# Reordering the recurrent stage of a hybrid decoder step: lagged page values, sample tokens inside turns, twelve value places

## The chip, the cores and the metric

The kernel runs on one core of one Trainium2 chip. The metric is device time in microseconds (us) of one execution. The engines are named as the profile names them: PE (TensorE matmul), PEld (its weight load), DVE (VectorE), ACT (ScalarE), POOL (GpSimd) and SP (SyncE, which issues DMAs only). Each engine executes its own queue strictly in the order in which the program wrote it; semaphores join the queues.

## The reference, cut to what matters

One inference step of a two-layer decoder trunk, for 1024 prompt tokens and 8 sample tokens with the same weights. Layer 0 joins stick-breaking attention and a matrix-state recurrence (RWKV-7) in one projection; layer 1 is a gated DeltaNet; each layer ends in a convolutional feed-forward part. The change is in layer 0's recurrent stage, in which two things are computed side by side.

```python
# (a) the recurrence, 8 heads, state 64 x 64 per head, over the 1024 prompt tokens, and one step for each sample
def step(s, inp):
    r_t, w_t, k_t, v_t, kk_t, a_t = inp
    sa = einsum('bhvk,bhk->bhv', s, kk_t)
    s = s * w_t - sa (x) (kk_t * a_t) + v_t (x) k_t
    return s, einsum('bhvk,bhk->bhv', s, r_t)
# then per head: group norm of o, + bonus = sum(r*k*r_k) * v, times the gate g = sigmoid(xg) @ g_up

# (b) stick-breaking attention of each sample token over 8192 past positions in 64 pages of 128
z = q . k * scale + bias                      # 64 key pages, 8 heads
u = log_sigmoid(-z); after = reverse cumulative sum(u) - u
w = exp(log_sigmoid(z) + after)
o = sum over pages of w @ v                   # 64 value pages
```

## The kernel before, in words

The recurrent stage is `rwkv_phase` (L1367). It cuts the 1024 prompt tokens into NPAIR = 8 blocks of W = 128 tokens and runs turns i = 0 to 8. In turn i, block i is "local": its Gram matrices are formed, and a triangular system is solved by doubling in five levels (`solve_y`, `solve_z`, DVE `level`, L2027). Block i-1 is "walked": the state is read, changed and multiplied out in two half steps p = 0, 1 (`state_read`, `new_values`, `change_and_outputs`, DVE `state`, L2036), then normed and gated (`center`, `normed`, `outputs`). Block i+1 is "prepared": gates, decays and keys are computed (`gate_ones` to `bonus`, DVE). The semaphore `solved` is counted by the DVE's last `level` (the second L2034 row of level 5), and PE's next `turn` (transposes, L1507) waits for it.

Between these steps lie the samples' cache pages, one sample per turn. A page is 128 positions x 512 floats, 256 KB.

- Key pages: SP loads them into 8 places (`load_keys`, L1008). DVE multiplies two pages by the sample's query (L1103) and sums (L1106) into scores `pg_z`. Such a pair is a unit; a turn takes KEYS_TURN = 26 units, spread by calls `more(n)`, the rest after the last level. All 256 units are done before turn 7; turn 6 gets the last 18.
- Page weights: DVE adds the bias (L1118), ACT takes three activations (`logs_act`, L1072 to L1074), DVE forms the softplus `pg_sp` (L1123), PE two running sums (`sums_pe`, L1030 and L1031), DVE four operations (`exponents_dve`, L1130 to L1133), and ACT the exponential `pg_w` (L1078). Sample i+1's weights are made at the end of turn i; sample 0's before turn 0.
- Value pages: POOL loads them into RING = 8 places (`load_values`, L1060, DMA at L1065), each behind a wait for the place's release by PE. PE multiplies four pages at a time (`values_pe`, L1035, matmul L1044; `more(4)` in PE's list). Sample i's 64 pages are all multiplied in turn i, the rest after the last `solve_z`. Then ACT copies the sum out (`fold_act`, L1083, which waits for the 64th page), PE selects (L1051, `select_pe`), and ACT picks (L1090), all before the next turn's transposes.

POOL also loads each block's projected rows X (L1456), from one place in its list; the first one, the LoRA weights and the first eight value pages are loaded once the stage has begun.

The 8 sample tokens are a ninth block. It is prepared in turn 7. After turn 7's last value page its rows are transposed (L1639), copied, written to memory and read back in another layout (SP, L1432 to L1437); nine DVE operations make its state step (L1931 on `pg_k`, L2160, L2167), and the result goes through memory again (L1443, L1447) to be normed, gated and written to `h`. Then the output projection (`residual_phase`) begins.

What stands between "engine", "line" and "operation" in a row is the program's name of the tile; many DVE operations go through the helper `tt` and so all bear L1931.

Of the kernel before, what the change touches and what calls it, by code (L numbers as in the profile page):

```python
# [14 lines left out]
F32 = mybir.dt.float32  # L15
# [6 lines left out]
P = 128  # L22
D_MODEL = 1024
SEQ = 1024
# [931 lines left out]
class Pages:  # L956
# [3 lines left out]
    RING = 8  # L960
    ZRING = 4
    UNITS = NPG // 2

    def __init__(self, T, ctx):
# [4 lines left out]
        self.v_in = [sems(f"v_in{n}") for n in range(self.RING)]  # L969
# [7 lines left out]
        self.kp, self.vp = sb("_k", [P, self.RING, D_A]), sb("_v", [P, self.RING, D_A])  # L977
# [5 lines left out]
        self.zb, self.sp, self.tmp, self.cum = (sb(n, [P, H_A * NPG]) for n in ("_zb", "_sp", "_tmp", "_cum"))  # L983
# [4 lines left out]


# [31 lines left out]
    def start_pe(self, pe):  # L1021
        pe.wait_ge(self.qc_in, 16)
        for t in range(4):
            mm = pe.transpose(self.T.ps[0:NS, 7, t * P:(t + 1) * P], self.qc[:, t, :], self.T.const("ident"))
        mm.then_inc(self.q_turned, 1)
        pe.sem_inc(self.v_used, self.RING)
# [6 lines left out]
    def values_pe(self, pe, b, pages):  # L1033

        wts = self.wts[:, b % 2, :].rearrange("p (h n) -> p h n", h=H_A)  # L1035
        for at in range(0, len(pages), 4):
            four = pages[at:at + 4]
            if four[0] == 0:
                pe.wait_ge(self.w_ready, b + 1)
            for g in four:  # L1040
                pe.wait_ge(self.v_in[g % self.RING], 16 * (NPG // self.RING * b + g // self.RING) + 16)
            for g in four:
                c = 32 * (g % 4)
                pe.matmul(self.T.ps[c:c + H_A, 7, :], wts[:, :, g], self.vp[:, g % self.RING, :], start=(g < 4),  # L1044
                          stop=(g >= NPG - 4), tile_position=(0, c), skip_group_check=True).then_inc(self.v_used, 1)
# [15 lines left out]
    def load_values(self, pool, b, g):  # L1061

        pool.wait_ge(self.v_used, NPG * b + g + 1)
        page = pool.value_load(self.table[0:1, NPG * b + g:NPG * b + g + 1], min_val=0, max_val=self.T.n_phys - 1)
        pool.dma_start(self.vp[:, g % self.RING, :], self.T.io["v_pages"][bass.ds(page, 1), :, :]  # L1065
                       .rearrange("a p n -> (a p) n")).then_inc(self.v_in[g % self.RING], 16)

    def logs_act(self, act, b):
# [3 lines left out]
        st.link(act.activation(self.tmp[:, :], self.zb[:, :], ACT.Abs))  # L1072
        st.link(act.activation(self.tmp[:, :], self.tmp[:, :], ACT.Exp, scale=-1.0))
        act.activation(self.tmp[:, :], self.tmp[:, :], ACT.Ln, bias=1.0).then_inc(self.logged, 1)  # L1074

    def weights_act(self, act, b):
        act.wait_ge(self.z_ready, b + 1)
        act.activation(self.wts[:, b % 2, :], self.cum[:, :], ACT.Exp).then_inc(self.w_ready, 1)  # L1078

    def fold_act(self, act, b):  # L1080
        act.wait_ge(self.v_used, self.RING + NPG * b + NPG)
# [33 lines left out]
    def bias_dve(self, dve, b):  # L1115
        assert self.unit >= self.UNITS * (b + 1)
        dve.wait_ge(self.reduced, self.UNITS * (b + 1) + 1)
        dve.tensor_tensor(self.zb[:, :].rearrange("p (h n) -> p h n", h=H_A), self.z[:, b % self.ZRING, :, :],  # L1118
                          self.T.vec("sb_bias").unsqueeze(2).to_broadcast([P, H_A, NPG]), ALU.add).then_inc(self.biased, 1)

    def softplus_dve(self, dve, b):
        dve.wait_ge(self.logged, b + 1)
        dve.scalar_tensor_tensor(out=self.sp[:, :], in0=self.zb[:, :], scalar=0.0, in1=self.tmp[:, :], op0=ALU.max,  # L1123
                                 op1=ALU.add).then_inc(self.softplus_ready, 1)

    def exponents_dve(self, dve, b):

        st, ps, run = Steps(dve, self.step, 3 * b), self.T.ps, self.tmp[:, :]
        dve.wait_ge(self.summed, b + 1)
        st.do(dve.tensor_tensor(self.cum[:, :], self.zb[:, :], ps[:, 6, :], ALU.subtract))  # L1130
        st.link(dve.tensor_tensor_scan(run, self.T.const("scanhead"), ps[:, 5, :], 0.0, ALU.mult, ALU.add))
        st.link(dve.tensor_tensor(run, run, ps[:, 5, :], ALU.subtract))
        dve.tensor_tensor(self.cum[:, :], self.cum[:, :], run, ALU.subtract).then_inc(self.z_ready, 1)  # L1133


KEYS_V, KEYS_PB, KEYS_ATT, KEYS_TURN = 16, 42, 24, 26


def attention_phase(T):
# [23 lines left out]
    with ExitStack() as ctx:  # L1163
# [12 lines left out]
        def _(pool):  # L1176
            for i in range(2):
                for u in range(2):
# [9 lines left out]
                      .then_inc(heads_in[u], 16)  # L1188

# [176 lines left out]

def rwkv_phase(T):  # L1367

# [1701 lines left out]
```

## Time and profile before

| | |
|---|---|
| three timed runs | 4803.83, 4805.32 (median), 4811.03 us |
| the profiled execution's own time | 4802.16 us |
| its span, first to last instruction | 4800.6 us |
| mean granted PE clock | 0.869 of 2.4 GHz |
| busy over the span | PE 3889.0, PEld 3356.1, DVE 2353.2, ACT 1177.8, POOL 399.9 us |
| the recurrent stage | about 697 to 1713 us of the span |
| value page DMAs, key page DMAs | 512 of 256 KB each kind, landing in 4.6 and 4.3 us (medians) |

Rows of the trace give a start and a duration in us from the span's start. An idle time in square brackets is that of the engine just before the row, with what ended it. PE's clock is the granted share of 2.4 GHz in a stretch, and takes the levels 1.2 and 2.4 GHz. A matmul row may join several instructions ("x8"), since an fp32 matmul is issued in two passes.

### The profile page before, as it was taken

The numbers are of one execution on the slowest core, as the hardware profiler recorded it, in microseconds if no ns is written. First come the engines' busy times: TensorE is split into PE (matmuls) and PEld (weight loads), VectorE is DVE, ScalarE is ACT, GpSimd is POOL, SyncE is SP. The second block draws the span as 40 slices with busy tenths as digits, with TensorE's granted clock in tenths as the row PEclk, the third lists the DMA queues.
The fourth block names the chain that finished last, engine by engine and source line by source line (L and its number), as shares of the span: only waits on it lengthen the run. The fifth ranks groups of instructions, "written<-read, shape, count | busy, mean of one in ns | idle before, by whom it ended". The sixth has DMA issues, their size and how long they took to land. (4 is left out here: it accounts for less than half of the span.)

```text
span 4800.6 us, 77677 instructions
## 1 busy us (share of the span) xinstructions
PE 3889.0 (81%) x29645; PEld 3356.1 (70%) x29645; DVE 2353.2 (49%) x3055; ACT 1177.8 (25%) x1872; POOL 399.9 (8%) x737
## 2 busy tenths in 40 slices
PE   6897875666666766999999699969888376999999
PEld 5695323344344466999999589857777276999999
DVE  2488878777775243344421345444444533434511
ACT  3223661222222112222310222222222012222300
POOL 0010003223223100000000000000000000000000
PEclk8998987777778688999999899977777588999999
DMA  2464227788776322111122222211010132111122
GB/s 95 154 208 148 75 72 262 267 270 271 270 267 219 105 102 76 51 46 44 45 76 69 96 89 80 85 45 36 19 36 10 43 137 75 44 44 53 43 77 66
DMA packets 212082, 512.43 MB, mean 107 GB/s; under 512 B 34129, under 2 KB 67297, under 8 KB 205274
## 3 DMA queue, kind: packets, MB, share of 16 engines
q1 hardware_dynamic: 149338, 305.83, 19.6%
q0 software_dynamic: 62496, 203.32, 12.4%
q8 instruction: 152, 2.49, 0.2%
q14 instruction: 96, 0.79, 0.0%
HBM read 454.87 MB, written 54.56 MB: 106 GB/s over the span
## 5 line engine op out<-in xcount | busy, mean ns | idle before, releaser
L263 PE MATMUL ps<-ffn_hh,up_wh 128*128 128x344 f32 x2112 | 678.3, 321 | 59.6 <-DVE up_wl L255 59.6
L265 PE MATMUL ps<-ffn_hl,up_wh 128*128 128x344 f32 x2112 | 676.7, 320 | 0.0
L264 PE MATMUL ps<-ffn_hh,up_wl 128*128 128x344 f32 x2112 | 675.9, 320 | 0.0
L263 PEld LDWEIGHTS ps<-ffn_hh,up_wh 128*128 128x128 f32 x2112 | 398.5, 189 | 60.7 <-issue 60.7
L265 PEld LDWEIGHTS ps<-ffn_hl,up_wh 128*128 128x128 f32 x2112 | 398.4, 189 | 0.0
L264 PEld LDWEIGHTS ps<-ffn_hh,up_wl 128*128 128x128 f32 x2112 | 398.4, 189 | 0.0
L458 PE MATMUL ps<-down_ah,down_wh 128*128 128x344 f32 x1056 | 343.2, 325 | 29.6 <-DVE down_al L492 18.1
L459 PE MATMUL ps<-down_ah,down_wl 128*128 128x344 f32 x1056 | 340.0, 322 | 0.0
L460 PE MATMUL ps<-down_al,down_wh 128*128 128x344 f32 x1056 | 339.9, 322 | 0.0
L1103 DVE TENSOR_TENSOR pg_prod<-pg_k,pg_q 128x1024 f32<-128x1024 f32 x256 | 313.4, 1224 | 40.0 <-DVE rw_mxt L2034 10.7
L1065 POOL DMA_DIRECT2D pg_v<-in_v_pages x512 | 275.8, 539 | 601.9 <-issue 467.0
L1106 DVE TENSOR_REDUCE pg_z<-pg_prod 128x16 f32<-128x1024 f32 x256 | 312.9, 1222 | 8.8
L1044 PE MATMUL ps<-pg_v,pg_w 128*8 128x512 f32 x1024 | 170.3, 747 | 173.2 <-DMA pg_v<-in_v_pages 170.5
L263 PE MATMUL ps<-hh,odd_wh 128*128 128x344 f32 x792 | 258.4, 326 | 63.9 <-DVE odd_wl L255 63.9
L265 PE MATMUL ps<-hl,odd_wh 128*128 128x344 f32 x792 | 254.9, 322 | 0.0
L264 PE MATMUL ps<-hh,odd_wl 128*128 128x344 f32 x792 | 254.8, 322 | 0.0
L458 PEld LDWEIGHTS ps<-down_ah,down_wh 128*128 128x128 f32 x1056 | 200.6, 190 | 34.2 <-issue 29.2
L459 PEld LDWEIGHTS ps<-down_ah,down_wl 128*128 128x128 f32 x1056 | 201.6, 191 | 0.0
L263 PEld LDWEIGHTS ps<-hh,odd_wh 128*128 128x128 f32 x792 | 150.5, 190 | 72.6 <-ACT odd_row L2233 42.0
L460 PEld LDWEIGHTS ps<-down_al,down_wh 128*128 128x128 f32 x1056 | 200.7, 190 | 0.0
L255 DVE TENSOR_TENSOR down_wl<-down_w,down_wh 128x896 fp32r<-128x896 f32 (+1 forms) x48 | 54.3, 1135 | 280.2 <-ACT down_wh L250 280.2
L663 DVE TENSOR_TENSOR ffn_a<-up_cv,ps 128x344 f32 (+1 forms) x132 | 67.3, 510 | 246.7 <-PE ps L265 246.7
(415 smaller groups left out, 7370.6 us busy)
## 6 DMA issues: line engine op xcount, KB each, us to landing
pg_k<-in_k_pages SPq DMA_DIRECT2D x512, 256.0 KB, 4.3
pg_v<-in_v_pages POOLq DMA_DIRECT2D x512, 256.0 KB, 4.6
up_w<-in_w_ff SPq DMA_DIRECT2D x44, 1034.0 KB, 4.8
odd_w<-in_w_odd SPq DMA_DIRECT2D x33, 526.0 KB, 4.0
scratch_odd_rows<-odd_cv POOLq DMA_DIRECT2D x32, 516.0 KB, 4.5
down_w<-in_w_down SPq DMA_DIRECT2D x32, 448.0 KB, 3.4
dn_x<-scratch_odd_rows SPq DMA_DIRECT2D x8, 1536.0 KB, 7.8
scratch_x<-out_x POOLq DMA_DIRECT2D x16, 516.0 KB, 3.0
```

The lines of the kernel that those rows point to most:

```text
L255: dve.tensor_tensor(lo, w, hi.bitcast(F32), ALU.subtract).then_inc(rest_ready, 1)
L263: pe.matmul(out, wh, xh, start=(k == 0), stop=False)
L264: pe.matmul(out, wl, xh, start=False, stop=False)
L265: mm = pe.matmul(out, wh, xl, start=False, stop=(k == n - 1))
L458: pe.matmul(out, hi, ah[:, k, g[c]], start=(k == 0), stop=False)
L459: pe.matmul(out, lo, ah[:, k, g[c]], start=False, stop=False)
L460: mm = pe.matmul(out, hi, al[k][:, g[c]], start=False, stop=(k == FT - 1))
L663: dve.tensor_tensor(a[:, bass.ds(2 * i + j, 1), col].rearrange("p a t -> p (a t)"), cv[:, j, col], ps[:, 3 + c, 0:GC], ALU.mult).then_inc( ...
L1044: pe.matmul(self.T.ps[c:c + H_A, 7, :], wts[:, :, g], self.vp[:, g % self.RING, :], start=(g < 4), stop=(g >= NPG - 4), tile_position=(0, ...
L1065: pool.dma_start(self.vp[:, g % self.RING, :], self.T.io["v_pages"][bass.ds(page, 1), :, :] .rearrange("a p n -> (a p) n")).then_inc(self. ...
L1103: dve.tensor_tensor(self.prod[:, :, :], self.kp[:, at:at + 2, :], self.q[:, b % 2, :].unsqueeze(1).to_broadcast([P, 2, D_A]), ALU.mult).th ...
L1106: dve.tensor_reduce(self.z[:, b % self.ZRING, :, g:g + 2].rearrange("p h n -> p n h"), self.prod[:, :, :].rearrange("p n (h d) -> p n h d" ...
```

## The change

Everything is inside the stage and in what feeds it.

1. Page weights. Softplus of sample i, its sums and exponents move from the end of turn i-1 into the first third of turn i; the bias and ACT's logarithms stay at the end of turn i-1. The arithmetic is done in place in `zb` and `sp`.
2. Values lag. PE multiplies pages 0 to 47 of sample i in turn i (`new`, twelve groups of four, from the lora products on) and pages 48 to 63 in turn i+1 (`old`, four groups, in the first third). Fold, select and pick follow in turn i+1.
3. VRING = 12 value places. The first twelve pages, the first X, the LoRA weights and the samples' rows are loaded by POOL at the end of its list in the attention phase, into tiles opened before that phase.
4. Sample tokens. Their preparation, now in small tiles of their own, lies in turn 0; their rows go to memory and back by DMAs that ACT issues in turns 0 and 1; the nine DVE operations take the `more` places of turn 7, where there are no keys left. Their norm and gate lie between the last block's state steps.
5. Keys. KEYS_TURN is 25, the units are laid as 3, 2, 1, 2, 2, 1, 2, 2, 2, 2 and 6, and DVE's last level stands before the last six units and before the bonus and the outputs.

The core of the diff:

```diff
+    VRING = 12
-    def values_pe(self, pe, b, pages):
+    def values_pe(self, pe, b, four):
...
+        if four[0] == 0:
+            pe.wait_ge(self.w_ready, b + 1)
+            if b:
+                pe.wait_ge(self.folded, b)
-KEYS_V, KEYS_PB, KEYS_ATT, KEYS_TURN = 16, 42, 24, 26
+KEYS_V, KEYS_PB, KEYS_ATT, KEYS_TURN = 16, 42, 24, 25
...  # attention_phase, POOL
+            pool.dma_start(T.rw_X[:, :, :], T.xs_rows.rearrange("t p n -> p t n")[:, :, 0:2 * C]).then_inc(T.rw_x_in, 16)
+            pool.dma_start(T.rw_lora[:, :], io["w_lora"]).then_inc(T.rw_lora_in, 16)
+            pool.dma_start(T.rw_XS[:, :, :], T.xs_rows.rearrange("t p n -> p t n")[:, :, SEQ:TOK]).then_inc(T.rw_xs_in, 16)
+            pages.load_values(pool, range(Pages.VRING))
...  # rwkv_phase, PE
+                rest = iter(range(NPG - 16, NPG, 4))
+                begun = iter(range(0, NPG - 16, 4))
+                old = lambda: pages.values_pe(pe, i - 1, four(next(rest))) if walk else None
+                new = lambda: pages.values_pe(pe, i, four(next(begun))) if local else None
...
+                old()
                 if local:
                     grams_b(i)
+                    page_sums(i)
...  # rwkv_phase, ACT
                 if local:
                     copy_y(i, 1)
+                    pages.weights_act(act, i)
...
+                if walk:
+                    pages.fold_act(act, i - 1)
                     copy_values(i - 1, 1)
...  # rwkv_phase, DVE
+                pages.softplus_dve(dve, i)
+                more(3)
+                blocks_t(i)
                 more(2)
                 if walk:
                     state(i - 1, 0)
+                blocks(i)
+                pages.exponents_dve(dve, i)
...
+                level(i, 5)
+                if ahead and not first:
+                    bonus(i + 1)
+                if walk:
+                    outputs(i - 1, h[:, 4:8, (i - 1) * W:i * W])
+                if ahead:
+                    more(KEYS_TURN - 19)
                     pages.bias_dve(dve, i + 1)
```

The first place is PE at the boundary from turn 1 to turn 2. Before, from the matmul of the bonus sums (L1499) to the first value group of turn 2:

```order
L1499 MATMUL ps<-rw_t,consts 128x512
L1044 MATMUL ps<-pg_v,pg_w 8x512 x4
L1030 MATMUL ps<-pg_sp,consts 128x512
L1031 MATMUL ps<-pg_sp,ones_sb 128x512
L1537 MATMUL ps<-rw_mxm,rw_mmt 64x64 x16
L1044 MATMUL ps<-pg_v,pg_w 8x512 x8
L1537 MATMUL ps<-rw_mxt,rw_my 64x64 x16
L1044 MATMUL ps<-pg_v,pg_w 8x512 x4
L1051 MATMUL ps<-consts,pg_fold 128x2 x4
L1507 MATMUL ps<-consts,rw_K 128x128 x4
```

In the change, the last rows of a turn and the first of the next (L1048 are values, L1587 a level, L1557 transposes):

```order
L1587 MATMUL ps<-rw_mxt,rw_my 64x64 x16
L1048 MATMUL ps<-pg_v,pg_w 8x512 x8
L1557 MATMUL ps<-consts,rw_K 128x128 x4
L1557 MATMUL ps<-consts,rw_e 128x128 x4
L1557 MATMUL ps<-consts,rw_xs 128x128 x4
```

and a little later in the same turn, from the end of the state read to the state change:

```order
L1048 MATMUL ps<-pg_v,pg_w 8x512 x4
L1565 MATMUL ps<-rw_AR,rw_e 64x128 x16
L1033 MATMUL ps<-pg_sp,consts 128x512
L1034 MATMUL ps<-pg_sp,ones_sb 128x512
L1626 MATMUL ps<-rw_ur,rw_mxt 64x64 x8
L1048 MATMUL ps<-pg_v,pg_w 8x512 x4
L1636 MATMUL ps<-rw_mvtm,rw_mktm 64x64
```

The sums on `pg_sp` have left the end of the turn, and the select on `pg_fold` no longer stands before the transposes.

The second place is DVE from a turn's first key units to the level-0 copy after the state step. Before, in a middle turn:

```order
L2011 COPY_PREDICATED rw_mxt<-consts,ps 128x512
L1931 TENSOR_TENSOR rw_mrb<-ps,consts 128x512
L1103 TENSOR_TENSOR pg_prod<-pg_k,pg_q 128x1024
L1106 TENSOR_REDUCE pg_z<-pg_prod 128x2x8
L1931 TENSOR_TENSOR rw_dh<-rw_Hx,ps 64x256 x2
L1931 TENSOR_TENSOR rw_Hx<-rw_dh,rw_eend 64x4x64 x2
L2018 COPY_PREDICATED rw_mxm<-consts,ps 128x512
```

In the change (L2120 is the old L2011, L1130 the softplus; three key units, L1108 and L1111, stand between the softplus and L2120):

```order
L2120 COPY_PREDICATED rw_mxt<-consts,ps 128x512
L2033 TENSOR_TENSOR rw_mrb<-ps,consts 128x512
L1108 TENSOR_TENSOR pg_prod<-pg_k,pg_q 128x1024
L1111 TENSOR_REDUCE pg_z<-pg_prod 128x2x8
L1108 TENSOR_TENSOR pg_prod<-pg_k,pg_q 128x1024
L1111 TENSOR_REDUCE pg_z<-pg_prod 128x2x8
L2033 TENSOR_TENSOR rw_dh<-rw_Hx,ps 64x256 x2
L2033 TENSOR_TENSOR rw_Hx<-rw_dh,rw_eend 64x4x64 x2
L2127 COPY_PREDICATED rw_mxm<-consts,ps 128x512
L1137 TENSOR_TENSOR pg_zb<-pg_zb,ps 128x512
```

Two units instead of one stand between the first copy and the state step, and the exponents follow it.

The third place is DVE in turn 7 of the change, where the samples' state operations (on `pg_k`) stand between the last block's levels (L2140, L2143):

```order
L1130 SCALAR_TENSOR_TENSOR pg_sp<-pg_zb,pg_sp 128x512
L2033 TENSOR_TENSOR pg_k<-pg_k,rw_kv 128x2048
L2120 COPY_PREDICATED rw_mxt<-consts,ps 128x512
L2033 TENSOR_TENSOR rw_mrb<-ps,consts 128x512
L2187 TENSOR_REDUCE rw_kv<-pg_k 128x32
L2033 TENSOR_TENSOR rw_dh<-rw_Hx,ps 64x256 x2
```

Before, all of them stood behind the last block's outputs to `h`:

```order
L1931 TENSOR_TENSOR h<-rw_oc,ps 128x4x128
L1931 TENSOR_TENSOR pg_k<-pg_k,rw_mmt 128x2048
L2160 TENSOR_REDUCE rw_mmt<-pg_k 128x32
L1931 TENSOR_TENSOR pg_k<-pg_k,rw_mmt 128x2048
L1931 TENSOR_TENSOR pg_k<-rw_mmt 128x2048
```

## Rows read from the trace of the kernel before

**Rows 1.** Stretches: span; busy us of PE, PEld, DVE, ACT, POOL; PEclk, DMA share, GB/s.

```profile
728.00:844.00 116.00, 67.13 (x803) 37.53 (x801) 97.42 (x100) 23.31 (x42) 38.24 (x69) 0.76 0.84 283
960.00:1076.00 116.00, 73.09 (x934) 46.79 (x935) 92.96 (x101) 24.57 (x45) 34.41 (x64) 0.76 0.80 266
```

**Rows 2.** Waits of VectorE, 960 to 1192: us in total, times, longest us.

```profile
DVE rw_dh L1931 <- PE ps L1596: 23.4, 2, 12.3
DVE rw_mxt L2011 <- PE ps L1515: 7.7, 2, 4.5
```

**Rows 3.** Timeline of VectorE: first copy of turns 0, 1, 5 and 7 (start, us).

```profile
738.40 0.74 DVE L2011 COPY_PREDICATED rw_mxt<-consts,ps 128x512 f32<-128x512 int32 x1 [0.18 <-PE ps L1515]
...
843.17 0.75 DVE L2011 COPY_PREDICATED rw_mxt<-consts,ps 128x512 f32<-128x512 int32 x1 [3.00 <-PE ps L1515]
...
1317.73 0.75 DVE L2011 COPY_PREDICATED rw_mxt<-consts,ps 128x512 f32<-128x512 int32 x1 [4.80 <-PE ps L1515]
...
1549.28 0.75 DVE L2011 COPY_PREDICATED rw_mxt<-consts,ps 128x512 f32<-128x512 int32 x1 [20.20 <-PE ps L1515]
```

**Rows 4.** Timeline of PE, the end of turn 2's solve and values.

```profile
1052.68 2.08 PE L1030 MATMUL ps<-pg_sp,consts 128*128 128x512 f32 x2 [17.29 <-DVEq L2004]
...
1067.60 1.91 PE L1044 MATMUL ps<-pg_v,pg_w 128*8 128x512 f32 x8 [6.67 <-DMA pg_v<-in_v_pages]
1072.16 1.83 PE L1051 MATMUL ps<-consts,pg_fold 128*128 128x2 f32 x8 [2.66 <-ACT pg_fold L1083]
1073.86 1.09 PE L1507 MATMUL ps<-consts,rw_K 128*128 128x128 f32 x4
```

**Rows 5.** Timeline of VectorE, turn 2: bias, last level and the key unit behind it.

```profile
1038.08 0.68 DVE L1118 TENSOR_TENSOR pg_zb<-pg_z,vecs_sb 128x512 f32<-128x512 f32 x1
...
1061.10 0.72 DVE L2034 COPY_PREDICATED rw_mxt<-consts,ps 128x512 f32<-128x512 int32 x1
1062.13 1.23 DVE L1103 TENSOR_TENSOR pg_prod<-pg_k,pg_q 128x1024 f32<-128x1024 f32 x1 [0.31 <-DVE rw_mxt L2034]
...
1064.74 1.23 DVE L1103 TENSOR_TENSOR pg_prod<-pg_k,pg_q 128x1024 f32<-128x1024 f32 x1
```

**Rows 6.** Timeline of ScalarE: last logarithm of turn 2.

```profile
1040.12 0.63 ACT L1074 ACTIVATE pg_tmp<-pg_tmp 128x512 f32<-128x512 f32 x1
```

**Rows 7.** Timeline of GpSimd: value loads of turn 2, and of turn 7.

```profile
1040.02 0.54 POOL L1065 DMA_DIRECT2D pg_v<-in_v_pages  x1 [0.62 <-issue]
1060.17 0.54 POOL L1065 DMA_DIRECT2D pg_v<-in_v_pages  x1 [19.62 <-PE ps L1044]
...
1558.30 0.54 POOL L1065 DMA_DIRECT2D pg_v<-in_v_pages  x1 [0.62 <-issue]
```

**Rows 8.** Stage's start: POOL's memset, ACT's first exponential, DVE's softplus.

```profile
698.62 0.54 POOL L1460 MEMSET rw_Hx<- 128x512 f32 x1
...
704.91 0.31 ACT L1745 ACTIVATE rw_eg<-rw_xs 64x128 f32<-64x128 f32 x1 [6.77 <-DMA rw_xs<-scratch_xs_rows]
...
725.30 0.69 DVE L1123 SCALAR_TENSOR_TENSOR pg_sp<-pg_zb,pg_tmp 128x512 f32<-128x512 f32 x1
```

**Rows 9.** Stage's end on PE: last values, second half step, samples' return.

```profile
1624.00 1.91 PE L1044 MATMUL ps<-pg_v,pg_w 128*8 128x512 f32 x8 [0.92 <-DMA pg_v<-in_v_pages]
...
1653.78 1.96 PE L1574 MATMUL ps<-rw_mr,rw_mxt 64*64 64x64 f32 x16 [0.68 <-ACT rw_mr L1817]
...
1707.98 0.59 PE L1731 MATMUL ps<-consts,pg_fold 8*128 8x8 f32 x4 [34.84 <-DMA pg_fold<-scratch_rw_o]
```

**Rows 10.** Stage's end on VectorE: last level, last block's output, samples' state, output.

```profile
1623.12 0.72 DVE L2034 COPY_PREDICATED rw_mxt<-consts,ps 128x512 f32<-128x512 int32 x1 [13.56 <-PE ps L1537]
...
1675.99 0.69 DVE L1931 TENSOR_TENSOR h<-rw_oc,ps 128x512 f32<-128x512 f32 x1
1676.90 2.29 DVE L1931 TENSOR_TENSOR pg_k<-pg_k,rw_mmt 128x2048 f32<-128x2048 f32 x1 [0.22 <-DVE h L1931]
...
1713.07 0.19 DVE L1931 TENSOR_TENSOR h<-rw_oc,ps 128x32 f32<-128x32 f32 x1
```

More of the change, by code:

```diff
@@ new lines, in bonus, with page_sums @@
+                pe.matmul(ps[:, 6, 0:4 * n], halves, cut(of(i)["t2"], n), start=True, stop=True).then_inc(S["bonus"], 1)
+            def page_sums(i):
+                if i == 0:
+                    pe.wait_ge(S["bonus_used"], 1)
+                    pe.wait_ge(S["k_rn"], 1)
+                else:
+                    pe.wait_ge(S["bonus_used"], prep(SMP if i == 1 else i) + 1)
+                    if i >= 2:
+                        pe.wait_ge(S["finished"], norm(i - 2) + 1)
+                pages.sums_pe(pe, i)
@@ L1791, in eyes @@
+                last.then_inc(S["decays"], 1)
             def eyes(i):
@@ L1870, in _ @@
                     token_major(i)
[L1871 to L1873 removed]
                 if walk:
                     copy_read(i - 1, 0)
[L1876 to L1877 removed]
+                else:
+                    sample_rows(0)
                 if walk:
@@ new lines, in _ @@
+            pages.bias_dve(dve, 0)
+            gate_ones(0)
+            tanh(0)
+            keys(0)
+            lora_bias(0)
+            sigmoid_ones(0)
+            log_decays(0)
+            modified_keys(0)
+            products(0)
+            bonus(0)
+            samples = sample_state()
+            for i in range(NPAIR):
+                walk, ahead, last, first = i >= 1, i + 1 < NPAIR, i + 1 == NPAIR, i == 0
+                def more(n):
+                    if last:
+                        next(samples, None)
+                    else:
+                        pages.keys_dve(dve, n)
+                pages.softplus_dve(dve, i)
+                more(3)
+                blocks_t(i)
@@ L2107, in _ @@
+                if ahead:
+                    gate_ones(i + 1)
+                if first:
+                    gate_ones(SMP)
+                more(2)
+                level(i, 1)
+                if ahead:
                     tanh(i + 1)
+                    if first:
+                        tanh(SMP)
                     keys(i + 1)
-                    level(i, 1)
-                    more(1)
+                if first:
+                    keys(SMP)
+                more(2)
+                if ahead:
@@ L2172, in rwkv_phase @@
+            for _ in samples:
+                pass
+            state(7, 0)
+            center(SMP, ocol[:, :, :])
+            normed(SMP)
+            state(7, 1)
+            outputs(SMP, h[:, 4:8, SEQ:TOK])
+            center(7, o)
+            normed(7)
+            outputs(7, h[:, 4:8, 7 * W:8 * W])
     sems.clear()
     pages.sems.clear()
+    T.rw_sems.clear()
 def odd_phase(T, ba):
```

739 lines of the change are left out of this document (391 added, 348 removed).

## The prediction, made before the run

> **What bounds the kernel now.** I read the stage by stretches first, then the waits of the engine that is busiest there, then its timeline, turn by turn. The stretches [rows 1] show a middle turn: in 116 us DVE is busy 93, PE 73 at a granted clock of 0.76, and the DMA engines 0.80 of the time. No engine is full, so a turn is a chain that passes from one engine to the other. Its length is read from one mark, DVE's first copy of each turn [rows 3]: turn 0 takes 843.17 - 738.40 = 104.8 us, turns 1 to 4 take (1317.73 - 843.17) / 4 = 118.6 each, and turns 1 to 6 together 1549.28 - 843.17 = 706.1. DVE's own waits over two turns [rows 2] are 23.4 us for the state change (L1596) and 7.7 for the Gram matmuls (L1515), so 15.6 a turn; without them a turn is 118.6 - 15.6 = 103.0 us of DVE work laid end to end, with its small gaps. Turn 0 has no state to walk, and its 104.8 is near that.
>
> Why does DVE wait? PE arrives late at the turn's front. In turn 2 [rows 4] PE stood 17.3 us until its sums' turn came, since the PSUM bank that they need is freed by DVE's bonus; behind them it stood 6.7 us for value pages, then 2.7 for the fold, and made its transposes at 1073.86. But DVE had finished the last level at 1061.8 [rows 5]. So 12 us lie between "solved" and the next turn's first transpose, in which PE only brings the old turn's pages home. POOL stood 19.6 us in the same time for want of a free place [rows 7] and otherwise issues one page every 1.16 us, 0.54 of work and 0.62 between two: that is the rate of the value stream, 4.6 us for a group of four.
>
> At the end of the stage the critical path leaves DVE: from the last level at 1623.1 to the samples' output at 1713.3 [rows 10] lie 90 us, of which 34.8 PE waits for the samples' state to come back through memory [rows 9].
>
> **The change part by part.** The sum is made against the profiled execution: 4802.16 us, span 4800.6. The median of the timed runs is 3.2 us above it.
>
> Start. ACT's first exponential stood at 704.91 for X; now the memset that ends at 699.16 releases it, -5.7 [rows 8]. The softplus of sample 0, before at 725.30, then ends at 725.99 - 5.7 = 720.3. The exponents no longer stand in front of the keys; three key units follow. A unit is 1064.74 - 1062.13 = 2.61 us [rows 5]. So turn 0's mark comes at 720.3 + 7.8 = 728.1, if PE's transposes, Gram and sums fit below it (they have 8 us), against 738.4: -10.3.
>
> Turn 0. Before 104.8. One unit less, -2.6; the 3.0 wait at its end goes [rows 3]; the new wait for the logarithms comes. Its price: the bias ends at 1038.76 and ACT's last logarithm at 1040.75 [rows 5, 6], so DVE, which now asks for the softplus right behind the bias, stands 2.0 us. The samples' preparation adds 14 small DVE operations of about 0.19 us (the size of the sample row at 1713.07 [rows 10]), 2.7. Their round trips over ACT and PE have no rows in such company; they cost between 0 (other work between) and about 6 us (four trips of 1.5); I take 3, since two of the four stand right behind one another. Sum 104.8 - 2.6 - 3.0 + 2.0 + 2.7 + 3.0 = 106.9. Turn 1's mark is at 835.0: -8.2.
>
> Turns 1 to 6. What moves: the last level now stands before the last six units, 15.7 us, and PE needs nothing more than that and the prepared block to make the next turn's transposes, the state's read and one group of old pages. It then stands, as before, but for DVE's softplus: 2.3 us of outputs, 15.7 of keys, 0.7 bias, 2.0 wait and 0.7 softplus, 21 us behind the level. ACT is held there too, since the eyes and the copies of the transposes stand behind the logarithms in its queue; that is what now releases the Gram matmuls. From there: Gram, sums, new values, four old pages, state change, some 14 us (2 + 4 + 2 + 2 + 4), while DVE has five units and two copies, 14.5. So the 12 us wait for the state shrinks to 0 to 2, and the 3 to 4 us wait for the Gram goes. In the second half PE must read twelve groups in about 50 us; POOL gives one in 4.6, three lie ready in the twelve places, and the other nine take 41.6 plus a landing of 4.6, so 46. The level that ends the turn needs only the tenth of them. This fits with a few us to spare. DMA: 64 value pages and 50 key pages of 256 KB, 30 MB, against 0.84 share for 283 GB/s [rows 1], 337 GB/s at a full share, is 89 us a turn: below it too.
>
> A turn is thus 103.0 - 2.6 (one unit) + 2.0 (softplus) = 102.4, plus what is late next: the second state step, pages that land late, keys that wait for a busier DMA. Between 0 and the 10 us of which the spare times above are made; I take 2.5, nearer to the lower end, because turn 0 before ran the same page and key traffic in 104.8 with its front not bound by it. 105 us, six turns 630 against 706.1 (whose last had eight units fewer but a wait of 20.2 [rows 3]). Turn 6 has one unit less and the load of the samples' state ahead of turn 7's mark; I set one against the other. Turn 7's mark: 835.0 + 630 = 1465 against 1549.3: -84.3.
>
> Turn 7 and the end. There the value stream binds. The first new group comes some 20 us behind the mark; three groups lie ready, and thirteen more (nine new, four old) need 13 x 4.62 = 60.1 us and a landing of 4.6: the last old group is there 85 us behind the mark, at 1550. The second half step of the last block follows it: matmul 1.9 (as at 1624.00), fold 2.7 [rows 4], then from new values to output as before, 1676.68 - 1653.78 = 22.9 [rows 9, 10], and the select 1.8: 29.3. The stage ends at 1465.0 + 84.7 + 29.3 = 1579.0 against 1713.3. The samples' nine DVE operations, of 2.29 us and more each, and their way through memory lie inside turn 7 beside the value stream; their 34.8 us wait goes. If they did not fit there, up to 10 us of it would come back.
>
> Sum: 1713.3 - 1579.0 = 134.3 less; 4802.2 - 134.3 = 4668 for such an execution, 4670 with half of the median's distance. Of it 8 are the start and turn 0 together, 76 the six turns, 50 turn 7 and the end. The twelve value pages, X and weights that are loaded in the attention phase, 4 MB, are in a stretch where POOL has nothing else; I cost them at nothing. Nothing outside the stage is touched.
>
> A rule that speaks against the change: while DVE runs an operation, POOL's loads might be held. Rows first: with DVE full of keys and the bias POOL's issue at 1040.02 took 0.54 and came 0.62 behind the one before; at 1558.30, with DVE standing, it was 0.54 and 0.62 again [rows 7]. The Trainium skill, SBUF — State Buffer, section "SBUF: two separate sides", says that a DMA issued from GpSimd can starve, as its descriptors cannot be written while DVE holds the shared port. By that rule a denser DVE would slow the value stream; the trace disagrees for the operations of this stage, and the sum stays without it.
>
> **The rivals.**
> (A) Turns stay PE's. For it: PE is busy 73 us [rows 1], would stand 17 in front, and if it still met 20 us of page waits (three of 6.7) and 5 of hand-overs, a turn is 115. Against it: the pages of the front have now had 20 us to land. Time: 4670 + 6 x 10 = 4730.
> (B) Turns reach the pure DVE work, 100.4 to 102: 4670 - 6 x 4 = 4646.
> (C) Slower than before: PE falls to the low clock for whole turns. The front wait grows from 17.3 to some 20 us together with ACT's, each followed by slow matmuls (the sums at 1052.68 took 2.08 us [rows 4]). The work of 73.09 us at 0.76 is 111 at 0.5; with 20 in front, a turn is 131. The point: start and end save 8.2 + 49.7 = 58 us, so it decides above 706.1 / 6 + 58 / 6 = 127.4 us a turn; at 131 the time is 4826. Against it: fewer page waits break PE's run in the second half.
> (D) The held value stream: by rows, 1.16 plus a key operation's 1.23 a page would be 153 us a turn, 4670 + 6 x 48 = 4958. The rows above exclude it nearly. The rule named above is this one.
>
> **How the numbers follow.** Forecast 76 in 100, A 12, B 8, C 3, D 1. B and the forecast's own lower side reach to 4640; on the upper side 112 us a turn (all spare times used up) gives 4712, and part of A belongs inside: 4640 to 4718. A measurement of this kernel tells about 0.2 %, 10 us, from no change. Forecast, A and B are all faster; C and D are slower, and only a sliver lies between: faster 0.95, same 0.01, slower 0.04.
>
> **What would show it.** Marks of DVE's first copy 104 to 107 us apart, the first at 728; the wait of the state operation under 3 us and a 2 us wait before each softplus; PE's wait in front of its sums 12 to 17 us; DVE busy over 0.9 of a turn; POOL at 1.16 us a page without a break in turn 7; the samples' state operations between the levels. It would be wrong if DVE still stood 10 us for the state, if PE's value rows of the second half stood over 5 us a turn for DMA and the last level came late by it, or if the end behind turn 7's mark were not near 114 us.

## The result, and the profile after

| | before | after |
|---|---|---|
| median of the timed runs | 4805.58 us (4 runs, 4803.83 to 4811.03) | 4679.2 us (4 runs, 4677.42 to 4686.42) |
| the profiled execution, its span | 4802.16, 4800.6 us | 4680.17, 4678.6 us |
| mean granted PE clock | 0.869 | 0.884 |

After takes 0.9739 of before, 95% interval 0.9725 to 0.9753: 126 us less. 4670 was predicted, within 4640 to 4718. A mark is, as in the prediction, the start of DVE's first copy of a turn, which opens that turn; a group is four value pages, multiplied by PE at once.

Two executions do not enter the stage at the same time (bias of sample 0: 696.89 before, 694.16 after, with nothing changed ahead of it but loads), so stretches are measured inside it: "start" is from that bias to turn 0's mark, "end" from turn 7's mark to the last write of `h`.

| stretch, us | before | after | change | predicted change |
|---|---|---|---|---|
| start | 41.5 | 30.1 | -11.4 | -10.3 |
| turn 0 | 104.8 | 106.1 | +1.3 | +2.1 |
| turns 1 to 6 | 706.1 | 629.0 | -77.1 | -76.1 |
| turn 7 and end | 164.0 | 126.8 | -37.2 | -50.0 |
| stage | 1016.4 | 892.0 | -124.4 | -134.3 |

The span is 122.0 us shorter: 124.4 from the stage, 2.7 from the entry, and 5.1 went the other way behind the stage, where the code is the same.

DVE's first copies of turns 0, 1, 2 and 7 after [rows 3 are those of before]; none stands for PE any more (before 3.0 to 20.2 us from turn 1 on):

```profile
724.31 0.71 DVE L2120 COPY_PREDICATED rw_mxt<-consts,ps 128x512 f32<-128x512 int32 x1
...
830.40 0.73 DVE L2120 COPY_PREDICATED rw_mxt<-consts,ps 128x512 f32<-128x512 int32 x1
...
935.99 0.77 DVE L2120 COPY_PREDICATED rw_mxt<-consts,ps 128x512 f32<-128x512 int32 x1
...
1459.41 0.73 DVE L2120 COPY_PREDICATED rw_mxt<-consts,ps 128x512 f32<-128x512 int32 x1
```

The marks between lie at 1042.11, 1147.69, 1253.68 and 1359.28: turns 1 to 5 take 105.8 us each, turn 6 100.1.

Waits of DVE and then of PE over two turns, 936 to 1147 (us in total, times, longest), against [rows 2]:

```profile
DVE rw_dh L2033 <- PE ps L1648: 6.6, 2, 3.3
DVE pg_sp L1130 <- ACT pg_sp L1079: 4.0, 2, 2.0
```
```profile
PE ps L1565 <- ACT rw_mvtm L1873: 23.8, 2, 11.9
PE ps L1048 <- DMA pg_v<-in_v_pages: 12.6, 6, 3.4
PE ps L1508 <- DVE rw_th L2043: 8.3, 2, 4.2
```

The wait for the state fell from 11.7 us a turn to 3.3, that for the Gram matmuls went, and the 2.0 us before each softplus came, as predicted. PE still stands 11.9 us a turn at the front, now for ScalarE's copy of the transposes, and 6.3 us for value pages. The stretches of one turn, of turn 7 to its last level, and of the end [rows 1 has the columns]:

```profile
936.00:1042.00 106.00, 73.02 (x960) 44.30 (x958) 92.66 (x101) 25.68 (x48) 35.61 (x65) 0.82 0.88 295
...
1459.00:1525.00 66.00, 55.05 (x838) 34.74 (x839) 38.57 (x35) 12.82 (x25) 24.81 (x46) 0.86 0.65 194
1525.00:1586.00 61.00, 49.48 (x316) 30.67 (x312) 8.86 (x19) 11.40 (x27) 9.70 (x18) 0.53 0.30 88
```

DVE is busy 92.66 of these 106 us. In a whole turn before (1082.2 to 1198.4) it was busy 94.56 of 116.2, with one key unit (2.5 us of work) more, so its work is the same. In the last stretch PE is busy 49 of 61 us at a granted clock of 0.53, that is nearly all of it at 1.2 GHz.

The start: the exponential follows the table load and no longer waits for X (6.77 in [rows 8]), and the softplus, which ended at 725.99 in [rows 8], ends at 716.78. Of the 9.2 us between, 2.7 are the stage's earlier entry:

```profile
694.12 1.28 ACT L1802 ACT_TABLE_LOAD   x1 [0.78 <-PEq L124]
695.42 0.31 ACT L1811 ACTIVATE rw_eg<-rw_xs 64x128 f32<-64x128 f32 x1
```
```profile
716.09 0.69 DVE L1130 SCALAR_TENSOR_TENSOR pg_sp<-pg_zb,pg_sp 128x512 f32<-128x512 f32 x1
```

The end, against [rows 9, 10]. PE's timeline: the first new group, five of the six new groups that stand for their pages, then the four old groups, of which the last two stand for nothing:

```profile
1480.80 1.07 PE L1048 MATMUL ps<-pg_v,pg_w 128*8 128x512 f32 x8
...
1506.04 1.07 PE L1048 MATMUL ps<-pg_v,pg_w 128*8 128x512 f32 x8 [2.37 <-DMA pg_v<-in_v_pages]
...
1512.80 1.91 PE L1048 MATMUL ps<-pg_v,pg_w 128*8 128x512 f32 x8 [3.69 <-DMA pg_v<-in_v_pages]
1516.15 1.91 PE L1048 MATMUL ps<-pg_v,pg_w 128*8 128x512 f32 x8 [1.44 <-DMA pg_v<-in_v_pages]
...
1521.53 1.91 PE L1048 MATMUL ps<-pg_v,pg_w 128*8 128x512 f32 x8 [1.57 <-DMA pg_v<-in_v_pages]
...
1530.51 1.90 PE L1048 MATMUL ps<-pg_v,pg_w 128*8 128x512 f32 x8 [3.87 <-DMA pg_v<-in_v_pages]
...
1537.77 1.90 PE L1048 MATMUL ps<-pg_v,pg_w 128*8 128x512 f32 x8 [0.42 <-DMA pg_v<-in_v_pages]
...
1542.35 1.90 PE L1048 MATMUL ps<-pg_v,pg_w 128*8 128x512 f32 x8 [0.78 <-DMA pg_v<-in_v_pages]
...
1551.64 1.91 PE L1048 MATMUL ps<-pg_v,pg_w 128*8 128x512 f32 x8
...
1559.14 1.91 PE L1048 MATMUL ps<-pg_v,pg_w 128*8 128x512 f32 x8
```

DVE in the same place: the last level, the first state change, and the last write, whose end is the stage's:

```profile
1525.39 0.75 DVE L2143 COPY_PREDICATED rw_mxt<-consts,ps 128x512 f32<-128x512 int32 x1 [15.50 <-PE ps L1587]
...
1551.25 0.87 DVE L2033 TENSOR_TENSOR rw_dh<-rw_Hx,ps 64x256 f32<-64x256 f32 x2 [23.55 <-PE ps L1648]
...
1585.47 0.69 DVE L2033 TENSOR_TENSOR h<-rw_on,ps 128x512 f32<-128x512 f32 x1
```

### The profile page after: what moved, and what is told of

Same layout as the page of the kernel before. It is cut to its first block and busy times, and to the rows that moved or that the text cites. A ratio compares the mean times of both kernels' runs of the same rounds, so it can differ in the third digit from the quotient of the medians.

```text
span 4678.6 us, 77751 instructions
## 1 busy us (share of the span) xinstructions
PE 3857.8 (82%) x29645; PEld 3332.9 (71%) x29645; DVE 2356.5 (50%) x3054; ACT 1174.9 (25%) x1872; POOL 401.3 (9%) x739
## 3 DMA queue, kind: packets, MB, share of 16 engines
q1 hardware_dynamic: 148306, 305.03, 20.2%
## 5 line engine op out<-in xcount | busy, mean ns | idle before, releaser
L458 PE MATMUL ps<-down_ah,down_wh 128*128 128x344 f32 x1056 | 342.0, 324 | 30.7 <-DVE down_al L492 18.2
L1108 DVE TENSOR_TENSOR pg_prod<-pg_k,pg_q 128x1024 f32<-128x1024 f32 x256 | 313.5, 1225 | 35.3 <-DVE rw_mxt L2143 4.6
L1111 DVE TENSOR_REDUCE pg_z<-pg_prod 128x16 f32<-128x1024 f32 x256 | 312.9, 1222 | 8.8
L1048 PE MATMUL ps<-pg_v,pg_w 128*8 128x512 f32 x1024 | 165.0, 721 | 57.7 <-DMA pg_v<-in_v_pages 57.6
```

The costliest lines, as they stand in the source:

```text
L458: pe.matmul(out, hi, ah[:, k, g[c]], start=(k == 0), stop=False)
L1108: dve.tensor_tensor(self.prod[:, :, :], self.kp[:, at:at + 2, :], self.q[:, b % 2, :].unsqueeze(1).to_broadcast([P, 2, D_A]), ALU.mult).th ...
L1111: dve.tensor_reduce(self.z[:, b % self.ZRING, :, g:g + 2].rearrange("p h n -> p n h"), self.prod[:, :, :].rearrange("p n (h d) -> p n h d" ...
```

## The experiments

All are the changed kernel with one edit, but for "after once more", which has none, and the last two rows, which join edits. They ran in four batches, each with runs of the kernel before beside it, so a ratio is to that kernel on the same chip; stretches are from each one's own trace. "Turns 0 to 6" is the time from turn 0's mark to turn 7's. The two measurements of the unchanged "after" differ by 0.0009 in the ratio (4 us), by 1.2 us in the turns and 0.5 us in the end: smaller differences say nothing.

| kernel | ratio to before | 95% interval | start | turns 0 to 6 | end | stage |
|---|---|---|---|---|---|---|
| after (first measurement) | 0.9739 | 0.9725 to 0.9753 | 30.1 | 735.1 | 126.8 | 892.0 |
| after once more | 0.973 | 0.9713 to 0.9747 | 30.1 | 733.9 | 126.3 | 890.3 |
| no early loads | 0.975 | 0.9735 to 0.9765 | 37.4 | 734.9 | 126.7 | 899.0 |
| 8 value places | 0.9869 | 0.9851 to 0.9888 | 30.1 | 793.4 | 140.2 | 963.7 |
| 10 value places | 0.9755 | 0.9741 to 0.9768 | 30.1 | 734.8 | 130.0 | 895.0 |
| no lag | 0.9863 | 0.9846 to 0.9879 | 30.1 | 772.5 | 144.7 | 947.4 |
| samples late | 0.9802 | 0.9787 to 0.9817 | 30.1 | 732.4 | 155.7 | 918.3 |
| last level late | 0.9735 | 0.972 to 0.975 | 30.1 | 735.2 | 127.1 | 892.5 |
| bias early | 0.9734 | 0.972 to 0.9748 | 30.1 | 729.1 | 126.6 | 885.9 |
| two queues | 0.9712 | 0.9698 to 0.9725 | 30.1 | 735.1 | 118.4 | 883.7 |
| less DVE work | 0.9677 | 0.9658 to 0.9695 | 30.1 | 703.9 | 124.8 | 858.9 |
| bias early and two queues | 0.9701 | 0.9683 to 0.972 | 30.1 | 726.0 | 108.8 | 865.0 |
| the same, 10 + 10 places | 0.9708 | 0.9688 to 0.9729 | 30.1 | 725.2 | 120.5 | 875.8 |

**No early loads.** X, the LoRA weights, the samples' rows and the first value pages are loaded once the stage has begun, as before.

```diff
-            pool.dma_start(T.rw_X[:, :, :], ...)      # these four at the end of the attention phase
-            pool.dma_start(T.rw_lora[:, :], io["w_lora"])
-            pool.dma_start(T.rw_XS[:, :, :], ...)
-            pages.load_values(pool, range(Pages.VRING))
+            ...                                       # the same, at the head of rwkv_phase
```

> Against 4679 of the changed kernel. Undone: the loads of the first X, the LoRA weights, the samples' rows and the first twelve value pages in the attention phase; they are issued when the stage begins. My theory: only X is on the path, so turn 0's first copy on DVE comes 5 to 7 us later, everything after it is shifted by that, about 4685. Rival: the twelve pages' head start also counts, some 14 us of POOL's issue, 4693 or more. Second rival: other work hides it, 4679.

The first mark comes 37.4 instead of 30.1 us behind the bias, nothing else moves: 7.2 us, the upper end of what was expected. ACT's first exponential again waits for X:

```profile
701.90 0.31 ACT L1811 ACTIVATE rw_eg<-rw_xs 64x128 f32<-64x128 f32 x1 [7.22 <-DMA rw_xs<-scratch_xs_rows]
```

In the timed runs 7 us is 0.0015, and the intervals overlap, so that only the trace shows it.

**Eight value places.** `VRING = 8` in place of 12.

```diff
-    VRING = 12
+    VRING = 8
```

> Against 4679. Eight value places instead of twelve, all else as changed. My theory: the twelve groups of a turn's second part have one ready group less, the tenth lands 4.6 us later, which the turns' spare time takes up; turn 7 and the end, where the value stream binds, lose about one group: 4684 to 4690. Rival: the places are what made the turns short; each turn goes back by about 5 us, 4710 to 4715.

The theory failed, and the rival too was short of it: 0.9869 is 63 us above after's 0.9739 (of 4811), where the rival had 31 to 36. Turns 0 to 5 are 112 to 116 us, turn 6 is 109. Two turns' waits of PE and DVE (936 to about 1165):

```profile
PE ps L1048 <- DMA pg_v<-in_v_pages: 44.6, 12, 6.2
```
```profile
DVE rw_mxt L2143 <- PE ps L1587: 14.5, 4, 6.4
```

Of the twelve new groups the first starts 26.7 us behind the mark in both kernels (962.73 - 935.99; 976.40 - 949.71). From the first to the twelfth it is 1015.18 - 962.73 = 52.4 us with twelve places, 4.77 a group, but 1041.44 - 976.40 = 65.0 with eight, 5.91 a group. POOL's own rate is 4.64 for four. With eight places the four pages of a group are asked for only when the group two before it is used. They must be issued (4.6) and land (4.3, this run's median) before PE can use them: 8.9 us and a group's own matmul (1.1 to 1.9) for every two groups. That is an estimate of 5.0 to 5.4 each; what makes up the rest of the 5.91 is not shown. The last level of the solve, queued among the groups, comes late by it, and DVE with it.

**Ten value places.** `VRING = 10`.

> Ten value places instead of twelve; eight cost 64 us. Theory 1 (each place buys the time between a page's release and the next one's landing, in proportion): half of it, about 32 us, 4715 to 4722. Theory 2 (from some count on the places are enough, and twelve is past it): under 12 us, 4686 to 4698.

Theory 2: +3 us in the stage of the trace and +7.7 us by the ratio (+12 against "after once more"), where in proportion it would be 32. Nearly all that places can buy is bought with ten; whether more than twelve would buy anything was not tried.

**No lag.** All sixteen groups of a sample in its own turn; the four that lag are brought back.

```diff
-                rest = iter(range(NPG - 16, NPG, 4))
-                begun = iter(range(0, NPG - 16, 4))
-                old = lambda: pages.values_pe(pe, i - 1, four(next(rest))) if walk else None
+                rest = iter(())
+                begun = iter(range(0, NPG, 4))
+                old = lambda: None
 ...
-                new()
-                new()
+                for _ in range(6):
+                    new()
```

> Against 4679. No lag: all 16 groups of four value pages are multiplied in the sample's own turn, the last six behind the last solve; the page weights in the first third, the fold in the next turn and the rest stay as changed. My theory: PE stood 12 us in front of the Gram matmuls for ScalarE, and the extra groups fill that: turns 0 to 2 us longer, 4682 to 4695. Rival: the lag is the core of the gain, the 12 us between the last level and the transposes come back in each turn, about 4750.

0.9863, 60 us above after; turns of about 110 us. It stands nearer the rival. Turn 2 (mark 944.88) shows the sum: first group at 974.22, sixteenth at 1046.69, 15 x 4.83 us, and 9.1 to the next mark at 1055.78. The turn is now a stream of sixteen groups that must follow the weights. PE waits 41.8 us for pages between 936 and 1165, a little over two turns. This run moves only the pages; the weights stay where the change put them.

**Samples late.** DVE's nine operations for the samples' state stand behind the first half step of the last block instead of inside turn 7.

```diff
-                    if last:
-                        next(samples, None)
-                    else:
+                    if not last:
                         pages.keys_dve(dve, n)
 ...
-            for _ in samples:
-                pass
             state(7, 0)
+            for _ in samples:
+                pass
```

> Against 4679. The nine DVE operations of the samples' state step stand behind the last block's first half step instead of inside turn 7; PE waits for their way through memory in front of the second half step. My theory: their 23 us and the 8 us through memory come back nearly whole, the stage's end 30 us later, about 4710. Rival: the value stream, which ends late anyway, covers most of it, under 10 us, 4689.

As the theory had it: the end is 155.7 instead of 126.8 us, +28.9, and 0.9802 is 30 us above after. PE waits again for the samples' way through memory, 31.2 us, as in [rows 9]:

```profile
1579.97 0.59 PE L1728 MATMUL ps<-consts,rw_ksq 8*128 8x8 f32 x4 [31.19 <-DMA rw_ksq<-scratch_rw_o]
```

**Last level late.**

```diff
-                level(i, 5)
                 if ahead and not first:
                     bonus(i + 1)
 ...
                     more(KEYS_TURN - 19)
+                level(i, 5)
+                if ahead:
                     pages.bias_dve(dve, i + 1)
```

> In turns 1 to 6 VectorE does a turn's last six key units (15 us) ahead of the last level of the solve instead of behind it. Nothing on TensorE's queue waits for that level but the reads of the state a few steps into the next turn, and TensorE waits some 12 us a turn there for ScalarE anyway. My theory (the turn is bounded by VectorE's own work, and TensorE's slack at the turn's front takes the delay): 0 to 2 us a turn, 4682 to 4700 us on a chip where the kernel after takes 4686. Rival (the chain level, state read, new values has no slack left, as the runs with eight places and without the lag suggest): over 8 us a turn, above 4745.

The same time (0.9735; stage 892.5). Between 936 and 1147 PE's front wait of 11.9 us for ScalarE has become one for this level:

```profile
PE ps L1557 <- DVEq L2144: 27.2, 2, 14.0
```

So in turns 2 to 5, 105.6 to 106.1 us in both kernels, it is worth nothing where the level stands among the last keys: PE has no use for the 15 us that it gains. The equal sum hides two differences at the edges. Turn 0 takes 100.5 us instead of 106.1, since a wait of DVE goes that after has there,

```profile
802.93 0.73 DVE L2143 COPY_PREDICATED rw_mxt<-consts,ps 128x512 f32<-128x512 int32 x1 [6.70 <-PE ps L1587]
```

and turns 1 and 6 are 2.4 and 3.7 us longer.

**Bias early.**

```diff
                 if ahead:
+                    if i < 6:
+                        pages.bias_dve(dve, i + 1)
                     more(KEYS_TURN - 19)
-                    pages.bias_dve(dve, i + 1)
+                    if i == 6:
+                        pages.bias_dve(dve, i + 1)
```

> For the samples of turns 0 to 5 the bias of the next sample's page logits is taken ahead of a turn's last six key units (the units it needs are done by then), so ScalarE can take its three logarithm steps and go on to the next turn's copies 15 us earlier. My theory: VectorE's 2.0 us wait for the logarithm at a turn's front goes in six turns, and part of the 3.3 us wait for the first new state may: 12 to 25 us less, 4661 to 4674. Rival (another wait of VectorE takes its place, since TensorE's transposes and not ScalarE come last): 4682 to 4690.

The time is the rival's: 4683.79, where after would be 4682.3 to 4686.6 on that chip by its two ratios, so the timed runs show no gain. The trace says more. Over turns 0 to 6 DVE's wait for the logarithm went from 14.1 us (7 times) to 2.0, and 13.2 us of waits for key pages came, which after had at 1.0:

```profile
DVE rw_dh L2033 <- PE ps L1648: 18.4, 7, 4.1
DVE pg_prod L1108 <- DMA pg_k<-in_k_pages: 13.2, 11, 2.2
```

A removed wait was handed to the key stream. What is left in the trace is 5 to 6 us of the turns (729.1 against 733.9 and 735.1).

**Two queues.** For the last sample POOL issues the even value pages and SP the odd ones, each with semaphores of its own.

```diff
+            pages.load_values(sp, range(NPG * 7 + 1, NPG * 7 + 40, 2))
             sp.wait_ge(S["smp_done"], 1)
 ...
-            pages.load_values(pool, range(done, NPG * NS))
+            pages.load_values(pool, range(NPG * 7, NPG * 8, 2))
```

> The odd value pages of the last sample are issued by SyncE, idle then, and the even ones by GpSimd. In the kernel after TensorE waits 14 us for value pages in the last turn and behind it. Theory 1 (one queue's issue time of 1.16 us a page sets the end, as the prediction's end was counted): these waits go and the stage ends 10 to 14 us earlier, 4672 to 4676. Theory 2 (TensorE's own steps at the low clock and their exchanges with ScalarE and VectorE set it, and the pages' waits only lie between them): under 4 us, 4682 to 4686.

0.9712 is 13 us under the first measurement of after and 9 under the second; in the trace the end is 8.4 us shorter. PE's waits for pages there fell from 14.4 us to 7.9, 6.5 less; in after and in two queues:

```profile
PE ps L1048 <- DMA pg_v<-in_v_pages: 14.4, 8, 3.9
```
```profile
PE ps L1049 <- DMA pg_v<-in_v_pages: 7.9, 4, 3.6
```

Between the theories, nearer the first: what page waits were taken away came off the end in full. But the four old groups cost what they did. The last of them starts 91.4 us behind the mark (1553.98 - 1462.56), not 85, and none of the four waits for a page: from the last new group's start (1526.66) to it are 27.3 us, in after 28.6.

**Less DVE work.** Leaves work out: every second key unit multiplies one page of two, from turn 1 on.

```diff
-            dve.tensor_tensor(self.prod[:, :, :], self.kp[:, at:at + 2, :], ...)
+            n = 1 if u >= 107 and u % 2 else 2
+            dve.tensor_tensor(self.prod[:, 0:n, :], self.kp[:, at:at + n, :], ...)
```

> Leaves work out: from the first turn's end on, every second key unit multiplies one page instead of two, which takes about 0.6 us off each of 12 or 13 units a turn, 7.6 us of VectorE's work in each of turns 1 to 6. Nothing else is changed. My theory (VectorE's own work sets turns 1 to 6, and the next limit is close behind): most of it, 4 to 7.6 us a turn, 25 to 46 us in all, of which the last may be cut off where TensorE's value groups come last (12 groups behind the weights need 52 us, on top of 27 us in front and 27 us to the next mark). Rival (the value stream or TensorE's own chain already sets the turn's length, with VectorE filled up to it): under 2 us a turn, under 12 us in all.

The multiplication takes 0.69 instead of 1.22 us, so 75 of them are 40 us less work. That is 6.7 a turn, and turns 1 to 6 take 100.0 us each instead of 104.8. Seven tenths of the work taken away come off the time, so DVE does set the turn. The other three tenths show that other limits are near. One is seen in waits of DVE for keys, 9.0 us over turns 0 to 6, where after has 1.0 and 2.6 in its two traces:

```profile
DVE pg_prod L1109 <- DMA pg_k<-in_k_pages: 9.0, 11, 1.4
```

**Both changes that helped.** The edits of "bias early" and of "two queues" together.

> The two changes that shortened the stage in their traces, together: the bias ahead of the last six key units (6 us less in the trace), and the last sample's odd value pages issued by SyncE (8 us less). If they add up: 14 us under the kernel after, 0.971 of the kernel before. If the first one's gain comes back as waits for value pages: 8 us, 0.9722.

They add up: 0.9701 against 0.973 for after on the same chip, 4668.81 us (4659.43 to 4671.7) against 4683.18 (4677.73 to 4685.13). The two ranges do not touch. Its ratio is the lowest of the kernels that leave nothing out, though the intervals do not part it from two queues alone or from the next. Its trace has the end 9.6 us shorter than two queues alone, with nearly the same page waits (8.5 us). The difference is the clock: the stretch from the last level, of two queues and then of both,

```profile
1527.00:1581.00 54.00, 47.62 (x300) 30.16 (x292) 6.88 (x16) 11.38 (x27) 2.77 (x6) 0.50 0.20 62
```
```profile
1521.00:1567.00 46.00, 37.99 (x300) 25.17 (x292) 6.90 (x16) 11.37 (x27) 2.42 (x5) 0.65 0.22 67
```

has the same 300 matmuls in 47.6 us of work at 0.50 and in 38.0 at 0.65. The gain lies between the last new group and the last old one:

```profile
1520.08 1.91 PE L1049 MATMUL ps<-pg_v,pg_w 128*8 128x512 f32 x8 [1.63 <-DMA pg_v<-in_v_pages]
...
1525.61 1.06 PE L1049 MATMUL ps<-pg_v,pg_w 128*8 128x512 f32 x8
1527.67 1.07 PE L1049 MATMUL ps<-pg_v,pg_w 128*8 128x512 f32 x8
1533.13 1.07 PE L1049 MATMUL ps<-pg_v,pg_w 128*8 128x512 f32 x8
1539.41 1.91 PE L1049 MATMUL ps<-pg_v,pg_w 128*8 128x512 f32 x8
```

These 19.3 us (1520.1 to 1539.4) have a granted clock of 0.85 and 18.2 us of PE's work. In the eleven other traces in which four groups lag, PE's work in the same list is 27.2 to 27.4 us, at 0.50; in two queues, where PE waits for nothing in it, that is also its length, 27.3 us. From the last old group to the end it is 27.0 us in all twelve. Why the clock rose again in this one execution, after waits much like those of two queues, no run shows. So the stage of this trace, 25 us shorter than that of "after once more", flatters the edits by about 9.6 us; the 14.4 us between the medians are the figure to go by.

**Both, with ten key and ten value places.**

> The kernel with both changes (bias early, two queues), with its twenty places shared out as ten for keys and ten for values in place of eight and twelve. With the bias early VectorE waited 9.9 to 13.2 us in turns 0 to 6 for key pages (1.0 before). Theory 1 (key pages are asked for too late, since a place comes free too late): these waits go and the turns shorten by up to 10 us, while ten value places cost some 3 to 8 us: 0.969 to 0.971 of the kernel before. Theory 2 (the key pages share DMA engines that are 0.88 busy with the value pages, and land late whenever they are asked for): the waits stay, and the two value places are missed: 0.971 to 0.973.

0.9708 cannot be told from 0.9701. The waits for keys are gone from the trace, so it was the places and not the DMA engines that held the keys (theory 1 in this), but the turns are as long as they were (725.2 against 726.0). In their stead DVE stands for the state and the level. In turns 0 to 6 it is 20.2 us for the state, against 16.2 in "both", and 9.5 against 5.6 for the level; from 725 to 1458, a little into turn 7:

```profile
DVE rw_dh L2044 <- PE ps L1659: 24.1, 9, 4.1
DVE rw_mxt L2154 <- PE ps L1598: 9.5, 3, 6.7
```

The end is 11.7 us longer than in "both". 1.8 us of it are page waits, and 8 lie between the last new and the last old group, where this trace has the low clock.

Not tried: twelve places in the kernel before (its memory has room for no more than eight), and the page weights moved back to the turn's end with the rest kept. What the early weights alone are worth stays open.

## Why the prediction was right, and where it was not

- **What bounds.** Right. DVE's work laid end to end, 102.4 us with the 2.0 of the softplus, plus 2.5 of late arrivals gave 105. Turns 1 to 5 are 105.8: without their waits of 3.3 and 2.0 they have 100.5 us of DVE's own, where the prediction's terms give 100.4. The run with less DVE work shows the bound itself, and that others are near. That the six turns meet 630 to 1 us is in part luck: turns 1 to 5 are 4 us over it together, and turn 6, set equal to the others, is 5.7 us shorter than they are.
- **Start.** Right: 10.3 predicted, 11.4 measured; 7.2 of it is the early X, priced at 5.7. The rest, 4.2, lies in the new order of softplus, keys and exponents, which no run took apart.
- **Turn 0.** 106.9 predicted, 106.1 measured, but by luck. After has a wait of 6.7 us for the last level there, shown above, which the sum lacks; before had one of 5.9 us for PE (L2018), which the sum took as work and which went. With the level late the wait is gone and turn 0 takes 100.5. Of the 3 us put for the samples' round trips the trace shows 2.0 as waits (1.6 for ScalarE, 0.4 for PE).
- **The state's wait to 0 to 2, the softplus's 2.0.** 3.3 and 2.0. The reason given for the first, that "the last level now stands before the last six units", is wrong: with that level behind them the time is the same. What is left is what was taken from before it, PE's stand for the sums' bank, the old pages and the fold [rows 4]. This is argued: no run puts one of these back alone. With the lag undone, two turns show 10.4 us of waits for the state instead of 6.6, and 6.0 for the Gram matmuls. That the level no longer matters also follows from ScalarE's copies, which now come last.
- **"This fits with a few us to spare."** Right for twelve places, and the rate was right (4.77 us a group against 4.62). But how far the spare time hangs on the places was not asked, and what was expected of eight places put the turns' loss at nothing: the page's round trip, issue and landing, was counted once a turn and not once for each pair of groups.
- **The end.** The step that failed: "the last old group is there 85 us behind the mark". It came 1559.14 - 1459.41 = 99.7 behind it. Of the 15.0 us, 1.4 are the first group's (21.4 instead of 20), 3.5 the next eleven (49.7 instead of 46.2: rate and waits), and 10.1 the four old groups: 28.6 us (1530.51 to 1559.14) where 18.5 were put. They were priced at the stream's 4.62 each, but in PE's list they lie between the steps of the state's walk, and PE is busy 27.3 of the 28.6 us at a granted clock of 0.50; the last two wait for no page. The prediction asked what brings the pages and did not price PE's own list at the low clock. That it is the clock, and not the length of the list, is shown by "both": there the same list takes 19.3 us at 0.85, near the 18.5. Behind it, 27.0 us came where 29.3 were put.
- **The samples in turn 7.** Right: their 34.8 us wait is gone, and putting them back costs 28.9.
- **Outside the stage** 2.4 us came back on balance of an entry 2.7 earlier and 5.1 lost later; no run ties it to the change. Of the 12.3 us by which this execution misses 4668, these are 2.4 and the end is 12.8; the rest of the stage was 2.9 us better than put.
- **The signs named in advance.** One sign of being wrong came: the end is 126.8 us and not near 114. PE's page waits are 6.3 us a turn, over the 5 named, but the last level of the middle turns does not wait for PE. The state's wait is 3.3, just over 3. PE's wait in front is 11.9, at the low edge of 12 to 17. DVE is busy 0.87 of a turn and not over 0.9; the prediction's own terms gave 0.88 (92.6 us of work in 105).
- **The rivals.** None came. B, the pure DVE work, would need its waits of 3.3, 2.0 and those for keys to go together, and two runs show that taking one calls up another. A did not come with twelve places, though turns of 112 to 116 us come with eight; C's low clock came only at the end; of D there is no sign, with POOL at 1.16 us a page while DVE multiplies keys (977.27 to 978.50). But the prediction reads the passage that it names for D (the Trainium skill, SBUF — State Buffer, section "SBUF: two separate sides") too widely. The passage speaks of DVE operations in a 2-port perf mode, and no run here shows that those of this stage are in one, so these rows do not speak against it:

```profile
977.03 0.54 POOL L1070 DMA_DIRECT2D pg_v<-in_v_pages  x1 [0.62 <-issue]
978.19 0.54 POOL L1070 DMA_DIRECT2D pg_v<-in_v_pages  x1 [0.61 <-issue]
```

## What to carry to other kernels

When a chain of engines is relaxed, name the work that each engine has of its own; the longest of them, here DVE's 102 us, is where the forecast starts, and a small test that takes some of it away shows how near the next limit is. For a ring of buffers, count the round trip (issue, landing, use) against the places: below it each place is dear, above it nearly free. At the end of a stage, where an engine does its list alone, price the list itself, at either level of the clock. And where single traces are compared, look at the granted clock first.

## What the hardware showed that was not expected

- The end's 300 matmuls took 38 us of PE's time in one execution and 47.6 in another of nearly the same code, with the granted clock at 0.65 and 0.50. In after a value group (one row of eight) takes 1.07 us at 1506.04 and 1.91 at 1512.80, behind a wait of 3.69, and 1.90 or 1.91 in all later ones but the one at 1525.58 (1.06), though PE is busy 49 of the last 61 us: the low clock there is worth about 10 us of the end, against 14.4 us of page waits.
- The ring's knee is sharp: in the traces eight places cost 72 us of the stage, ten 3.
